# Rotating the sparse attention's keys and first query inside the projections, and adding the compression's position terms on GpSimd inside the retention

## The reference

```python
        h = _rmsnorm(x, mix_norm[layer])
        proj = h @ w_in[layer]
        (q_a, kc_a, vc_a, ks_a, vs_a, kw_a, vw_a, g_a,
         q_r, k_r, v_r, g_r, g_merge) = jnp.split(proj, split_points, axis=-1)
        nsa_gates = jax.nn.sigmoid(g_a.reshape(B, S, G, Hg, 3).transpose(0, 2, 3, 1, 4))
        ...
    q = _rope(q, pos, ROPE_DIM, ROPE_THETA)
    k_slc = _rope(k_slc, pos, ROPE_DIM, ROPE_THETA)
    k_win = _rope(k_win, pos, ROPE_DIM, ROPE_THETA)
    ...
    def compress(tok, w1, w2):
        blk = tok[:, :, cmp_idx] + pos_emb
        blk = blk.reshape(B, G, n_cmp, CMP_BLOCK * dh)
        return jax.nn.gelu(blk @ w1) @ w2

    kc = _rope(compress(k_cmp, ck_w1, ck_w2), cmp_end, ROPE_DIM, ROPE_THETA)
    vc = compress(v_cmp, cv_w1, cv_w2)
```

## Time and profile before

| | us |
|---|---|
| median of 3 runs | 2847.47 (2846.86 to 2848.49) |
| the profiled execution | 2847.13 |
| its span in the trace | 2845.8 |
| outside the span | 1.3 |

### The profile page before, as it was taken

One profiled execution on the slowest core, in us unless ns is written; L12 is line 12 of the kernel. 1 busy time (PEld: TensorE's weight loads), 2 busy tenths in 40 slices (PEclk: granted clock), 3 DMA queues, 4 the chain that ended last, 5 costly groups with the idle time before them and its releaser, 6 DMA issues.

```text
span 2845.8 us, 30331 instructions
## 1 busy us (share of the span) xinstructions
PE 2675.6 (94%) x12126; PEld 2138.1 (75%) x12126; DVE 897.9 (32%) x1515; ACT 930.6 (33%) x1497; POOL 1280.4 (45%) x645
## 2 busy tenths in 40 slices
PE   8999999967998999999999999999977799899998
PEld 7888888754666887888887888877855587788886
DVE  4222111356663113444313554111046323311111
ACT  4223222134654223322223222223265423332221
POOL 4444444435774444444444444444433345344443
PEclk9999999988999999999999999998988899899999
DMA  4222323220002332355332554222200022123221
GB/s 161 96 97 89 97 96 115 93 71 1 1 1 61 95 97 85 133 186 191 125 95 89 181 178 172 94 85 67 96 21 1 27 93 88 57 94 102 93 91 61
DMA packets 87340, 261.51 MB, mean 92 GB/s; under 512 B 10528, under 2 KB 11808, under 8 KB 87200
## 3 DMA queue, kind: packets, MB, share of 16 engines
q1 hardware_dynamic: 83888, 255.46, 27.2%
q10 hardware_dynamic: 3312, 4.12, 0.5%
HBM read 257.44 MB, written 2.10 MB: 91 GB/s over the span
## 4 chain that ended last, share of the span: by engine, by line
PE 88%; DVE 5%; POOL 4%; ACT 2%; issue 1%; DMA 0%; POOLq 0%; DVEq 0%; ACTq 0%; SPq 0%
PE ps L262 77%; POOL prob L1535 2%; PE ps L273 1%; PE ps L1334 1%; PE ps L1691 1%; PE ps L1304 1%; PE ps L930 1%; PE ps L1291 1%; PE ps L298 1%; PE ps L871 0%; PE ps L1292 0%; PE ps L1656 0%; PE ps L878 0%; POOL prob_d L1982 0%; PE ps L1680 0%
## 5 line engine op out<-in xcount | busy, mean ns | idle before, releaser
L249 POOL TENSOR_TENSOR split_ring<-raw_ring,split_ring 128x1024 fp32r<-128x1024 f32 x416 | 1016.4, 2446 | 1240.6 <-ACT split_ring L242 1240.6
L262 PE MATMUL ps<-hs,split_ring 128*128 128x512 f32 x6240 | 1442.6, 392 | 32.3 <-DVE hs L352 9.0
L262 PEld LDWEIGHTS ps<-hs,split_ring 128*128 128x128 f32 x6240 | 1176.8, 189 | 290.1 <-issue 15.9
L242 ACT ACTIVATE split_ring<-raw_ring 128x1024 fp32r<-128x1024 f32 x416 | 437.2, 1052 | 504.3 <-PE ps L262 489.6
L262 PE MATMUL ps<-ffn_act,split_ring 128*128 128x512 f32 x2112 | 495.4, 396 | 0.0
L262 PEld LDWEIGHTS ps<-ffn_act,split_ring 128*128 128x128 f32 x2112 | 397.8, 188 | 97.0
L533 ACT ACTIVATE ffn_act<-tmp 128x512 fp32r<-128x512 f32 x88 | 55.7, 633 | 405.1 <-DVE tmp L571 405.1
L1535 POOL TENSOR_SCALAR prob<-prob,small 128x512 f32<-128x512 f32 (+3 forms) x128 | 140.7, 1119 | 60.6 <-DVE small L1579 60.6
L571 DVE TENSOR_TENSOR tmp<-ps,tmp 128x512 f32<-128x512 f32 x44 | 30.4, 691 | 312.2 <-PE ps L262 312.2
L262 PE MATMUL ps<-split_ring,hs 128*128 128x512 f32 (+1 forms) x480 | 101.3, 372 | 0.0
L262 PEld LDWEIGHTS ps<-split_ring,hs 128*128 128x128 f32 x480 | 85.4, 188 | 15.5 <-issue 0.5
(11 more groups left out here) (302 smaller groups left out, 2490.9 us busy)
## 6 DMA issues: line engine op xcount, KB each, us to landing
raw_ring<-in_wstream SPq DMA_DIRECT2D x380, 512.0 KB, 3.5
ada_w<-in_w_ada SPq DMA_DIRECT2D x96, 256.0 KB, 3.6
raw_ring<-in_wstream SPq DMA_DIRECT2D x32, 384.0 KB, 3.0
sq<-in_w_ada SPq DMA_DIRECT2D x48, 256.0 KB, 3.7
x<-in_x_t SPq DMA_DIRECT2D x4, 512.0 KB, 6.4
decay<-in_decay ACTq DMA_DIRECT2D x8, 256.0 KB, 2.7
out_t<-x SPq DMA_DIRECT2D x8, 256.0 KB, 2.0
raw_ring<-in_wstream SPq DMA_DIRECT2D x4, 304.0 KB, 2.8
```

Source lines behind the costliest of these rows:

```text
L242: nc.scalar.activation(self.split[:, s, 0, :], self.raw[:, s, :], ACT.Copy).then_inc(self.sem("unit_hi"), 1)
L249: nc.gpsimd.tensor_tensor(self.split[:, s, 1, :], self.raw[:, s, :], self.split[:, s, 0, :].bitcast(F32), ALU.subtract).then_inc(self.sem( ...
L262: mm = self.nc.tensor.matmul(out, lhs, rhs, start=first and j == 0, stop=last and j == 2)
```

## The change

Six things are moved; apart from one pair of copies merged into one and some instructions halved in size, no arithmetic goes or comes.

- **Rotations.** The two keys and query 0 are rotated during the last units of `a.in.vr` (`pe_n_first_rope`, `pool_n_first_cos`, `dve_n_first_rope`). Query 0 is rotated in place.
- **Position terms.** The 8 additions go from VectorE to GpSimd, behind its last retention product; key tokens first, each addition waiting for the one before. To make room, the tiles `cx` and `cxs` are placed anew, one for keys and one for values, and the moments move into `small`.
- **Parts.** The rounding and subtraction of `cx` become two halves, and TensorE begins on the key half. The splits of the keys and of query 0 go in between the weight splits of `a.cmp`.
- **First scores** come right behind the compression's products, ahead of the transposes of the hidden layer; compressed scores come after the rotation of the compressed key. The compression uses banks 6 and 7 alone.
- **Gates.** The sigmoid goes into `a.in.vr` on ScalarE, with a reload of the square root's table behind it.
- Two `meet`s are removed.

```diff
+            if (name, t, u) == ("a.in.vr", 1, 2):
+                self.pe_n_first_rope()
...
+            if (name, t, u) == ("a.in.vr", 0, 1):
+                nc.scalar.wait_ge(sem("tm_act"), at("tm_act", "a.in.vg", 0, 2))
+                nc.scalar.wait_ge(sem("tm_dve"), at("tm_dve", "a.in.vg", 0, 3))
+                nc.scalar.activation(self.gates[:, :, :], self.gates[:, :, :], ACT.Sigmoid)
+                nc.scalar.preload_act_table(ACT.Sqrt)
...
+    def pe_n_first_rope(self):
+        nc, sem, at = self.nc, self.sem, self.at
+        for kind in range(2):
+            self.pe_rope(("k", kind), self.pq[:, 10 + kind, :], self.perm_n[:, :], 2 + kind)
+        nc.tensor.wait_ge(sem("rope_sin"), at("rope_sin", "ret", 0, 0))
+        self.pe_make_q(0, 0)
+
+    def pool_n_first_cos(self):
+        for kind in range(2):
+            self.pool_rope(("k", kind), self.pq[:, 10 + kind, :], self.cos_n[:, :], self.tmp[:, 2 + kind, :])
+        self.pool_make_q(0, self.ssq)
+
+    def dve_n_first_rope(self):
+        for kind in range(2):
+            self.dve_rope(("k", kind), self.pq[:, 10 + kind, :], self.sin_n[:, :], 2 + kind, self.tmp[:, 2 + kind, :])
+        self.nc.vector.wait_ge(self.sem("q_cos"), self.at("q_cos", 0))
+        self.dve_q_sin(0, 0)
+        self.dve_q_rope(0, self.ssq)
...
     def pool_retention(self):
...
+        for kv in range(2):
+            if kv == 0:
+                nc.gpsimd.wait_ge(sem("roped"), at("roped", "ret", 3, 1))
+            else:
+                nc.gpsimd.wait_ge(sem("ret_scored"), at("ret_scored", 5, 2))
+            cx = self.cx[kv].rearrange("p (l c) -> p l c", c=2 * N_CMP)
+            for g in range(2):
+                rows = slice(64 * g, 64 * g + 64)
+                for par in range(2):
+                    nc.gpsimd.tensor_tensor(
+                        cx[64 * par:64 * par + 64, :, g * N_CMP:(g + 1) * N_CMP], self.shifted(self.pq[rows, 8 + kv, :], par),
+                        self.pos[rows, par, :].unsqueeze(2).to_broadcast([64, 16, N_CMP]), ALU.add).then_inc(
+                        sem("cx"), to("cx", kv, g, par))
+                    nc.gpsimd.wait_ge(sem("cx"), at("cx", kv, g, par))
...
     def act_compress(self):
...
+        units = self.units("a.cmp")
+        for kv in range(2):
+            nc.scalar.wait_ge(sem("cx"), at("cx", kv, 1, 1))
+            nc.scalar.activation(self.cxs[kv][0], self.cx[kv], ACT.Copy).then_inc(sem("cx_hi"), to("cx_hi", kv))
+            self.act_split(units[kv][2] + LOOKAHEAD)
+        nc.scalar.wait_ge(sem("cx_lo"), at("cx_lo", 1))
+        for kind in range(2):
+            self.act_split_k(("n", kind), self.pq[:, 10 + kind, :], self.k_hi_n[:, 2 * kind:2 * kind + 2, :])
+            self.act_split(units[2 + kind][2] + LOOKAHEAD)
+        self.act_q_hi(0)
+        for t, u, g in units[4:]:
             self.act_split(g + LOOKAHEAD)
+        self.act_ret_gained(7)
...
     def pe_compress(self):
...
+        self.pe_ret_turn(7, 6)
+        for kind in range(2):
+            nc.tensor.wait_ge(sem("k_lo_n"), at("k_lo_n", kind))
+        for i in range(5):
+            self.pe_n_scores(0, i)
         nc.tensor.wait_ge(sem("hid_rows"), at("hid_rows"))
+        nc.tensor.wait_ge(sem("gained"), at("gained", 7))
...
     def pe_nsa(self):
         nc, sem, at = self.nc, self.sem, self.at
-        for kind in range(2):
-            if kind > 0:
-                nc.tensor.wait_ge(sem("roped"), at("roped", "k", 0))
-            self.pe_rope(("k", kind), self.pq[:, 10 + kind, :], self.perm_n[:, :], 7)
-        self.meet(nc.tensor)
-        self.pe_make_q(0)
-        for i in range(5):
-            self.pe_n_scores(0, i)
+        nc.tensor.wait_ge(sem("kc_wide"), at("kc_wide", "k"))
         self.pe_cmp_scores(0)
```

## The result

| | us |
|---|---|
| before, median of 4 runs beside the changed kernel | 2847.98 (2846.86 to 2848.91) |
| changed, median of 4 runs | 2827.44 (2824.33 to 2828.53) |
| ratio | 0.9928, 95% interval 0.9915 to 0.9941 |
| changed, the profiled execution and its span | 2828.53, 2827.2 |

The changed kernel is faster by 20.5 us, 0.7%; 2826.5 had been forecast. The span of the profiled pair fell by 18.6 us only (2845.8 to 2827.2).

What follows compares the result with a forecast made beforehand. TensorE, busy 94% of 2845.8 us, was taken as the bound, so only its idle or slow time could be won. -24.2 + 2.6 + 1.0 = -20.6 us took 2847.13 to 2826.5, range 2814 to 2832 (0.88).

Steps and rivals of the forecast that it cites:

- The projections, +2.6: Last projection unit: three more permutation products cost TensorE 2.6 us; GpSimd's and VectorE's work beside them and the sigmoid cost 0.
- The retention, +1.0: Retention's last heads: two or three small VectorE TENSOR_SCALAR instructions held under GpSimd's additions, +1.0 us, bounds 0 and 5.4.
- The additions: Eight position-term additions on GpSimd behind its last retention product: 1.8 us each, from 582.0 to 596.4, covered by idle time.
- The cover: Slack between the additions' end and ScalarE's rounding: 5.5 us, gone when an addition takes over 2.5 us.
- its own rule of 8 us per further microsecond: Rival that GpSimd's additions don't fit: from 2.5 us each, every further microsecond on all eight costs 8; slower 0.04.
- The compression and the scores: Retention's end to the loop's first transpose: compression starts at 602.1, scores at 628.2, transpose at 643.5 instead of 667.73, -24.2 us.
- The turns between low parts and splits: Beside the compression: VectorE's low part waits for a whole GpSimd split (2.35 us) and delays the next by 0.3 to 0.4.
- The first rival: VectorE not held by splits, or several low parts per gap: scores start at 620.7 at full clock, 2816.8 us; chance 0.20.
- The sum: Whole kernel: -24.2 + 2.6 + 1.0 = -20.6 us, from 2847.13 to 2826.5; chance 0.58.

Runs made afterwards that it cites:

- e4_splits_after_low_parts: Changed kernel with GpSimd's three splits for the stage after the sparse attention held until VectorE's low part of the first q: median 2818.72 us, ratio to before 0.9898.
- the best version: Changed kernel with first-step low and high parts first, one late split behind q's low part, two after the sparse loop: median 2815.38 us, ratio to before 0.9887.
- e10_rotations_in_gap: e9_parts_behind with the rotations of both keys and the first query also taken out of the projections, permutation products directly behind the retention: median 2822.99 us.
- e9_parts_behind: Changed kernel with high parts behind the hidden layer again, low parts and first scores behind the compressed key: median 2825.75 us, ratio to before 0.9925.
- e1_adds_on_dve: Changed kernel with the eight position-term additions put back on VectorE at the start of the compression: median 2833.54 us, ratio to before 0.9950.
- e2_adds_twice: Changed kernel with each of GpSimd's eight position-term additions made twice: median 2830.26 us, ratio to before 0.9937.
- e3_narrow_perms: Changed kernel with the three permutation products of the projections on 64 columns instead of 512: median 2824.52 us, ratio to before 0.9919.

## Why the prediction was right, and where it was not

**The projections, +2.6.** Measured 2.62 in every kernel with the three wide products there, gone in the one without. That the GpSimd and VectorE work beside the last unit costs nothing held too: its last instruction ended 0.4 us ahead of the retention's first scores. One reading was not exact: the addition of the earlier trace rows did not end with the split but 0.54 us behind it (538.84 against 538.30), as the held low parts do; no term of the sum hung on that.

**The retention, +1.0.** Measured 0.32 (50.96 to 51.28). The mechanism was right, the term too large: two of the small instructions fell under additions, one was held by 1.0, the other by nothing, and VectorE had 0.7 of that to spare before TensorE noticed. The page of the Trainium skill that I had weighed (SBUF — State Buffer, Who interferes with whom) says that an instruction in a two-port mode finds the pair locked until the other ends. The ends at 595.09, 599.33 and 603.3 agree, for an instruction of 4 elements with a step of two, which I had thought too small for it; what it costs is a question of slack behind it.

**The additions.** 1.26 us each and one every 1.34, near the lower bound of 1.23; the ratio of VectorE's own two access patterns (1.48), by which I took 1.8, does not carry over to GpSimd. Nothing hung on it, as 1.8 was covered too. The cover was said to be gone from 2.5 us each on; at 2.65 (each done twice) 2.0 us of loss by cause appeared, 1.2 of it ahead of the first unit. (For 6.5 us each the prediction gives 2857; by its own rule of 8 us per further microsecond it is 2858.5.)

**The compression and the scores.** The idle time of 3.9 us was exact. The first scores had been put at 628.2 on the clock of before; measured 632.13 less the 4.05 by which the retention ended later (602.25 against 598.20), 628.08. Five low parts were to be held in a row and the sixth, the last, to be free: so it was (five of 2.72 to 2.77 us, ending at 620.22 to 631.28, then one of 0.69). One more was held ahead of them (2.76, ending at 616.75). The granted clock in the scores, put at 0.5, was 0.62 (0.59 before). The scores took 5.5 us (5.65), and from them to the loop's transposes it was 9.2 (9.65). In sum 24.9 us gained instead of 24.2. The turns between low parts and splits, on which this rested, are shown by `e4_splits_after_low_parts`: with three splits away, 8.1 us went at once. The first rival (VectorE not held) did not come true in this kernel, but its estimate was about right for one in which the three late splits don't stand against the low parts: 9.65 us, measured 8.1, and 11.2 in the best version.

**The sum.** 2.6 + 0.3 - 24.9 = -22.0 in the middle columns, 1.4 more than forecast. The profiled execution gave back 1.1 us ahead of the change and 2.3 behind it, the second one took 1.0 less than before there. That the forecast's 2826.5 is so near the eight runs' 2826.2 is partly luck: single executions spread over 6 us.

**What the prediction did not see.** It followed the changed order step by step and got the time, but it never asked what each part of the change was worth by itself. The runs say:
- Additions off VectorE: 9.0 us of TensorE's idle time (12.95 to 3.92); put back they cost 7.3 us.
- Rotations and parts no longer strung one behind the other: from the compressed key (633.86) to the first scores (657.23) it was 23.4 us before, and 7.6 with the parts put behind again (628.49 to 636.08): 15.8 us. It is not the rotations' being in the projections: `e10_rotations_in_gap` has the same 7.6 us (626.01 to 633.61) with them elsewhere. A `meet` is a part of this: in the kernel before, the one between keys and query held the query's permutation until VectorE was done with the keys' low parts, 11.05 us of idling on TensorE, with 6.5 us of the query's own chain behind it (650.73 to 657.23, line below). No run puts the two `meet`s back alone, so how the 15.8 divide between them and the rotations' place is not shown.
- Parts beside the compression: nothing as it stands (44.6 against 44.1 us). What they save behind it they lose in turns with the splits. With the three late splits out of the way they do pay: 36.5 us.
- First scores ahead of the hidden layer: a loss of 1.6 us as it stands.

The query's permutation in the kernel before, with the wait that the `meet` made:

```profile
650.73 2.07 PE L1341 MATMUL ps<-pqr,perm_n 128*128 128x512 f32 x2 [11.05 <-DVEq L215]
```

9.0 + 15.8 makes 24.8 of the 25.4 us that `e9_parts_behind` gains up to the loop (69.52 to 44.11); the changed kernel gains 24.9. What stays open is whether the scores' place ahead of the hidden layer pays where the low parts are early, and why the clock falls in one execution and not in the next. In `e1_adds_on_dve`, `e2_adds_twice` and `e3_narrow_perms` it had fallen already in the compression's last two units (0.69, 0.69 and 0.60 on average, against 1.00 in both executions of the changed kernel), ahead of the wait for the scores; whether the edits or the execution did that is not shown, with one profile of each.

## What to carry to other kernels

When work is moved beside other work, ask whose instructions hold each other up: a split and a low part that take 2.34 and 0.69 us alone took 2.8 us together in turns, nearly the sum, and the first thing to move is the work that nobody waits for (three splits that were needed 220 us later cost 8 us here). After each such move look at what is next in the queue of the engine that was made to wait. And put each part of a change back alone: of the four parts that were put back here, only the additions' move was a gain (7.3 us); the parts' place beside the compression was worth nothing, the order of the scores cost 1.6 us and the rotations' place among the projections 2.8 us. The largest part of the gain, the 15.8 us behind the compressed key, was read from timelines alone.

## What the runs showed of the hardware that I had not expected

- A VectorE TENSOR_SCALAR of 4 elements per partition, 0.17 us, that starts under a GpSimd two-input instruction ends 0.03 us behind it: 1.17, 1.16, 1.01 and 0.89 us. The RECIPROCAL of the same size behind it was not held (0.18).
- GpSimd's addition of 64 x 496 elements, one input with a step of 16 elements, one broadcast: 1.26 us, against 1.27 for its contiguous product of 128 x 512. VectorE's took 0.99 against 0.70 for its contiguous ones.
- In a dense row of splits exactly one low part gets in per split: splits 2.8 us apart instead of 2.34, low parts 2.8 us apart instead of 0.70, each ending 0.54 us behind a split.
- The clock can cost more than the edit that is tested: the same instructions from the first scores to the loop took 14.7 us in the changed kernel, 16.3 in `e3_narrow_perms` and 17.7 in `e1_adds_on_dve` and `e2_adds_twice`.
